# A hybrid S5, attention and MoE step on one core: dense part reordered, x2 rows kept on chip, expert outputs split

## The chip, the core and the metric

The kernel runs on one core of a Trainium2 chip. The metric is the device time of one execution in microseconds. The kernel before has a median of 2260.08 us over three runs (2256.23 to 2265.83). The profile is of one further execution.

## What is computed

One decoder layer in float32 for a prompt of 512 positions and 8 single-token samples, 520 tokens of width 2048 in all:

```python
u, q, k, v = split(rmsnorm(x) @ w_in)          # S5 channels 1024, q, k, v 1024 each
q, k = rope(q), rope(k)
# S5: 64 groups of 16 channels, each with 64 complex states
xs = scan(lambda_bar, B_bar u);  y = Re(C xs) + D u
z = gelu(y);  z = z * sigmoid(z @ w_glu)
# attention: three dilated windows, merged by their denominators
o = merge(branch(q, k, v, w, d) for (w, d) in ((128,1), (512,4), (2048,16)))
x = x + concat(rmsnorm(z), rmsnorm(o)) @ w_out
h = rmsnorm(x)                                 # MoE: best group of 4, best 2 of its 8 experts
x = x + sum_j gate_j * ((silu(h @ w_g[e_j]) * (h @ w_u[e_j])) @ w_d[e_j])
y = rmsnorm(x)
```

The samples attend to 1024 cached keys and values of which 256 positions count, and start from given states. k, v and the last states are outputs too.

## The kernel before

Everything lies in one SBUF tensor, `arena`, cut by hand into regions (A, R, W, U, Q, K, V, X), and in the eight PSUM banks, `ps`. So the profile calls every operand arena or psum, and the lines tell the work apart. Each engine has its own program, ordered by hand; semaphores tie them. SP issues nearly all DMAs, in program order: a wait in front of one holds all that follow.

**Input projection.** w_in comes in 32 column tiles of 1 MB through a ring of two slots (`load_w`, `load_tiles`). PE multiplies each with the 520 normed columns of x (`product`, line 497, 64 instructions a tile; float32 runs as two passes). Tiles 0 to 7 give u, which DVE evacuates (`u_out`, lines 1127 to 1129); 8 to 31 give q, k, v, which ACT copies out (lines 856 to 858) and GpSimd rotates (lines 1026 to 1028, 1031). Meanwhile DVE and ACT compute lambda and its powers (lines 1134 to 1192), and GpSimd the injection weights (`complex_product`, lines 997 to 1002), ended by `s_bw`.

**Injection and scan.** The sequence is cut into 128 chunks of 4. ACT issues DMAs that stack the weights of four rounds on the partitions (`stack_weights`, line 823, 16 DMAs a round, in two buffers) and u (lines 844, 845). PE runs rounds 0 and 1 behind tile 9, rounds 2 and 3 behind tile 11 (`inject`, line 534); ACT evacuates them (`chunk_states`, lines 833, 834), and issues the stacking of round 2 between the evacuations of rounds 0 and 1. Then DVE scans the 128 chunks, four small operations each (lines 1206 to 1211). After the scan it computes the samples' states, copies the samples' q doubled (line 1235), and multiplies and reduces cached keys in 8 chunks (lines 1247, 1248), for which SP loads one chunk beside each w_in tile from 22 on; the load of chunk c waits until DVE has used chunk c - 2. PE turns the doubled q into rows (line 556) between tiles 21 and 22.

**Attention and readout.** Scores, mask, exp, transposes and weighted values run by head and query tile (lines 575 to 591, 1259 to 1270). GpSimd computes the powers of the readout weights meanwhile. PE then forms the lag kernels (line 611) and for each of 8 channel tiles the readout: products with the lag kernels (line 623), then 64 instructions in which 128 states go into 32 output partitions (line 629), and the samples (lines 632, 636). ACT applies gelu (lines 907, 908). DVE works on the samples' attention: the score maximum by way of PE, exp on ACT in front of channel tile 3's gelu, then cached values in 8 chunks (lines 1307, 1308).

**Gate and norms.** Eight products with w_glu (line 497), sigmoid (920), z2 = u * sigmoid (1319), squares (914) summed over partitions with a matrix of ones (658). Then z's root (925), reciprocal (1329) and mix (1331), the z half of output tiles 0 and 1, squares and sums of o, its root (929), reciprocal (1333) and mix (1335).

**Output projection and routing.** 16 tiles of w_out; DVE adds x (line 1340). PE transposes x2 to token rows (689) and multiplies with the router (694). ACT copies the rows out (936), SP stores them in four parts to `x2_rows` in HBM (`store_x2`). DVE computes the choice of experts, positions and block tables in many small linked operations (lines 1370 to 1452); GpSimd zeroes two row buffers (1085) once the stores have landed.

**Experts.** Blocks of up to 64 token rows, one or more for each of 32 experts. GpSimd gathers rows from `x2_rows` (1067), ACT scales them (954), PE transposes (747), multiplies with gate and up (767) and with down (783); GpSimd scatters to `y_rows` (1078). SP loads each expert's six chunks of 2 MB (lines 453, 456); chunk i waits until PE has used chunk i of the expert before.

**Tail.** When all is scattered, SP reads both outputs of each token (line 477), after its x2 rows (474). For each of five token tiles DVE adds two weighted outputs (1494, 1495), ACT takes the root (975, 977), DVE norms (1489, 1490), SP stores (482).

The engines that run these instructions take the quoted waits in order; the one around which part of the change turns is PE's, between w_in tiles 21 and 22:

```python
            proj_pairs(6, 11)

            pe.wait_ge(s_ex, 1)
            pe.wait_ge(s_injev, 24)
            mm(ps[:, 4, 0:DH], smp_p[:, 0:P], ident, start=True, stop=True).then_inc(s_rows, 1)
            proj_pairs(11, 16)
```

## Time and profile before

| | |
|---|---|
| median of three runs | 2260.08 us (2256.23 to 2265.83) |
| profiled execution, its time | 2255.8 us |
| its span, first to last instruction | 2253.9 us |
| mean granted TensorE clock | 0.916 |
| PE busy | 1830.0 us, 81% |
| DVE, ACT, GpSimd busy | 590.0, 309.3, 276.7 us |
| DMA | 540.38 MB, mean 240 GB/s |
| chain that ended last | DMA 36%, PE 32%, DVE 5% |

PE is TensorE's matmuls, PEld its weight loads, DVE VectorE, ACT ScalarE, POOL GpSimd, SP SyncE; ACTq and SPq are the issuing sides. A row of instructions gives start, duration, engine, line, operation, output and input, count, and in brackets the idle time before it and what ended that. The granted clock (PEclk) is the share of full speed, 2.4 GHz; 0.50 is the lower level, 1.2 GHz. A chain row gives the time by which an instruction extended the chain, often less than its own duration.

### The profile page before, as it was taken

The numbers are of one execution on the slowest core, as the hardware profiler recorded it, in microseconds if no ns is written. First come the engines' busy times: TensorE is split into PE (matmuls) and PEld (weight loads), VectorE is DVE, ScalarE is ACT, GpSimd is POOL, SyncE is SP. The second block draws the span as 40 slices with busy tenths as digits, with TensorE's granted clock in tenths as the row PEclk, the third lists the DMA queues.
The fourth block names the chain that finished last, engine by engine and source line by source line (L and its number), as shares of the span: only waits on it lengthen the run. The fifth ranks groups of instructions, "written<-read, shape, count | busy, mean of one in ns | idle before, by whom it ended". The sixth has DMA issues, their size and how long they took to land.

```text
span 2253.9 us, 27087 instructions
## 1 busy us (share of the span) xinstructions
PE 1830.0 (81%) x10962; PEld 1288.7 (57%) x10963; DVE 590.0 (26%) x1201; ACT 309.3 (14%) x509; POOL 276.7 (12%) x193
## 2 busy tenths in 40 slices
PE   7798996899669989999498787777787797977870
PEld 6687885787338878888354444444444454544430
DVE  6700899431963421000410000000000010100006
ACT  3002110001231120111111110110110111111102
POOL 0731322101830000000100000000000000000000
PEclk9899998899779999999789999898998999999995
DMA  5153122234912412222599999999999879899977
GB/s 215 57 147 97 67 74 93 76 150 150 13 40 92 170 38 75 75 94 75 194 361 399 415 409 409 398 402 391 398 394 397 342 276 415 338 404 415 412 325 300
DMA packets 92403, 540.38 MB, mean 240 GB/s; under 512 B 28760, under 2 KB 41560, under 8 KB 47256
## 3 DMA queue, kind: packets, MB, share of 16 engines
q1 hardware_dynamic: 69920, 516.23, 60.6%
q0 software_dynamic: 7776, 17.07, 2.4%
q10 hardware_dynamic: 14656, 6.33, 1.3%
q8 instruction: 39, 0.64, 0.1%
q14 instruction: 12, 0.10, 0.0%
HBM read 522.04 MB, written 30.91 MB: 245 GB/s over the span
## 4 chain that ended last, share of the span: by engine, by line
DMA 36%; PE 32%; DVE 5%; issue 2%; ACT 1%; SPq 0%; POOLq 0%; ACTq 0%; DVEq 0%
DMA arena<-w_up_in 34%; PE psum L497 13%; PE psum L767 10%; PE psum L629 2%; PE psum L783 2%; DVE arena L1267 1%; PE psum L623 1%; DMA arena<-y_rows 1%; PE psum L747 1%; DVE arena L1261 1%; PE psum L658 1%; DVE arena L1490 1%; PE psum L694 1%; DVE arena L1259 1%; DMA arena<-x_rows,arena 0%
## 5 line engine op out<-in xcount | busy, mean ns | idle before, releaser
L497 PE MATMUL psum<-arena 128*128 128x260 f32 x3328 | 753.7, 390 | 39.1 <-ACT arena L805 12.3
L497 PEld LDWEIGHTS psum<-arena 128*128 128x128 f32 x3328 | 645.1, 194 | 143.5 <-issue 28.7
L767 PE MATMUL psum<-arena 128*64 128x256 f32 x4352 | 540.6, 407 | 175.4 <-DMA arena<-w_up_in 142.4
L767 PEld LDWEIGHTS psum<-arena 128*64 128x64 f32 x4352 | 332.4, 147 | 393.5 <-DMA arena<-w_up_in 166.5
L783 PE MATMUL psum<-arena 128*64 128x512 f32 x1088 | 249.8, 612 | 20.1 <-ACT arena L963 15.7
L1480 DVE TENSOR_TENSOR arena<-arena,psum 128x256 f32<-128x256 f32 x34 | 14.3, 421 | 956.8 <-PE psum L767 956.8
L783 PEld LDWEIGHTS psum<-arena 128*64 128x64 f32 x1088 | 77.2, 140 | 170.8 <-issue 138.7
L1078 POOL DMA_INDIRECT y_rows<-arena x34 | 34.1, 1002 | 982.5 <-ACT arena L968 933.6
L963 ACT ACTIVATE arena<-psum 128x256 f32<-128x256 f32 x34 | 13.1, 384 | 498.5 <-PE psum L773 498.5
L747 PE MATMUL psum<-arena 64*128 64x64 f32 x560 | 69.6, 276 | 13.6 <-ACT arena L954 13.6
L747 PEld LDWEIGHTS psum<-arena 64*128 64x128 f32 x560 | 64.8, 202 | 26.8 <-issue 26.8
L954 ACT ACTIVATE arena<-arena 64x2048 f32<-64x2048 f32 x35 | 69.8, 1995 | 27.6 <-DMA arena<-x_rows,arena 25.1
L968 ACT ACTIVATE arena<-psum 128x512 f32<-128x512 f32 x68 | 36.9, 594 | 259.2 <-PE psum L783 259.2
L1340 DVE TENSOR_TENSOR arena<-psum,arena 128x520 f32<-128x520 f32 x16 | 11.2, 700 | 223.4 <-PE psum L497 223.4
L1206 DVE TENSOR_TENSOR arena<-arena 128x64 f32<-128x64 f32 x128 | 42.5, 332 | 92.6 <-ACT arena L834 82.1
L1085 POOL MEMSET arena<- 128x2052 f32 x2 | 3.6, 1825 | 467.1 <-DMA x_rows<-arena 467.1
L1458 DVE TENSOR_TENSOR arena<-psum,arena 128x512 f32<-128x512 f32 x70 | 48.4, 692 | 34.4 <-PE psum L747 34.3
L856 ACT ACTIVATE arena<-psum 64x520 f32<-64x520 f32 x16 | 9.6, 601 | 313.5 <-PE psum L497 185.5
L1026 POOL TENSOR_TENSOR arena<-arena 128x520 f32<-128x520 f32 x16 | 20.8, 1301 | 247.4 <-ACT arena L858 176.2
L583 PE MATMUL psum<-arena 128*128 128x128 f32 x80 | 20.1, 365 | 35.6 <-DVE arena L1270 35.6
L1211 DVE TENSOR_TENSOR arena<-arena 128x64 f32 x128 | 47.4, 370 | 4.4
L629 PE MATMUL psum<-arena 128*32 128x128 f32 x512 | 47.7, 273 | 0.0
(284 smaller groups left out, 1221.9 us busy)
## 6 DMA issues: line engine op xcount, KB each, us to landing
arena<-w_gate_in SPq DMA_DIRECT2D x64, 2048.0 KB, 28.2
arena<-w_up_in SPq DMA_DIRECT2D x64, 2048.0 KB, 27.9
arena<-w_down_in SPq DMA_DIRECT2D x64, 2048.0 KB, 26.6
arena<-w_in_in SPq DMA_DIRECT2D x32, 1024.0 KB, 4.8
arena<-w_out_in SPq DMA_DIRECT2D x16, 1024.0 KB, 4.8
arena<-k_cache_in SPq DMA_DIRECT2D x8, 1024.0 KB, 6.8
arena<-v_cache_in SPq DMA_DIRECT2D x8, 1024.0 KB, 4.8
arena<-y_rows SPq DMA_DIRECT2D x4, 2048.0 KB, 17.8
```

Source lines behind the costliest of these rows:

```text
L497: last = mm(pair(n)[:, h, :], w(kk), rhs(kk)[:, HALF * h:HALF * (h + 1)], start=(kk == 0), stop=(kk == kn - 1 and stop))
L623: mm(yjc[b][:, lag:CHUNK, :], lagk[:, ct, lag, :], ujc[:, ct, 0:CHUNK - lag, :], start=(lag == 0), stop=False, skip_group_check=True)
L629: mm(yjc[b][32 * r:32 * r + 32, j, :], cw[:, j + 1, ri, i, :], xs[:, ri, i, 0:NCH], start=False, stop=(j == CHUNK - 1 and ri == 1), skip_g ...
L747: last = pe.transpose(ps[:, 3 + g, CAP * m:CAP * (m + 1)], rows[:, 8 * g + m, :], ident[0:CAP, 0:CAP])
L767: last = mm(ps[64 * h:64 * h + 64, i // 2, 0:256], xtr[:, kk, :], w[:, kk, 256 * h:256 * (h + 1)], start=(kk == 0), stop=(kk == 15))
L783: last = mm(ps[64 * h:64 * h + 64, 5 + b, :], act_col[:, kk % 2, 64 * (kk // 2):64 * (kk // 2) + 64], wd[:, kk, 1024 * h + 512 * b:1024 * ...
L954: A(xsc[0:CAP], xrow[j][0:CAP, 0:DM], ACT.Copy, scale=xrow[j][0:CAP, DM:DM + 1]).then_inc(s_sc_x, 1)
L968: A(yrow[:, 512 * b:512 * (b + 1)], ps[:, 5 + b, :], ACT.Copy).then_inc(s_yv, 1)
L1078: pool.indirect_dma_start(out=y_rows, out_offset=bass.IndirectOffsetOnAxis(ap=idx_now[:, 2 + j:3 + j], axis=0), in_=yrow, in_offset=None, ...
L1206: tt(scan_t[:, 0], column(it * 4 + s), lam_same, ALU.mult).then_inc(s_scan, 1)
L1211: tt(column(it * 4 + (s + 1)), scan_t[:, 2], scan_t[:, 1], ALU.add).then_inc(s_scan, 1)
L1458: tt(xtr[:, 8 * g:8 * g + 8, :], ps[:, 3 + g, :].rearrange("p (k n) -> p k n", n=CAP), gtab[:, 8 * g:8 * g + 8].unsqueeze(2).to_broadcast( ...
```

## The change

- **Lambda** (the small operations of lines 1173 to 1192, in new scratch) moves behind the last evacuation of u and the end of the injection weights, with the zeroing of the u stack, which stood before the last evacuation. ACT no longer waits for lambda before it stacks weights.
- **Stacking of rounds 2 and 3** is issued by SP, between w_in tiles 11 and 12, instead of by ACT.
- **The scan** is split into two loops of 16 turns; the samples' doubled q is copied between them.
- **Lag kernels and readout**: the loop over the four quarters of 32 output partitions becomes the innermost.
- **Norms**: squares are added on DVE (two buffers), and PE sums each norm once. o's squares, adds, sum, root, reciprocal and mix stand inside the gate products; output tiles 0 and 1 begin with their o half.
- **Experts' scratch** moves from R to A, so that the x2 rows stay on chip to the end. GpSimd zeroes only the four last columns of its row buffers, once the router's logits are done.
- **First expert**: down chunks 0 and 1 and gate chunk 1 are loaded behind w_out tiles 4, 8 and 12.
- **Outputs by lower and higher expert**: ids and gates are swapped where the first choice has the higher number. At the end the lower experts' outputs are loaded once all blocks before the last expert's are scattered and the last gate chunk is used, and are added to x2 at once; the higher ones follow after the last scatter, the tile of 8 rows first. x2 is not read back.

```diff
-            load_tiles(2, 8)
+            load_tiles(2, 6)
+            for rd in (2, 3):
+                sp.wait_ge(s_inj, 6 * (rd - 1))
+                for r in range(4):
+                    for j in range(CHUNK):
+                        sp.dma_start(bws[rd % 2][32 * j:32 * j + 32, :, r, :],
+                                     bw[32 * r:32 * r + 32, CHUNK - 1 - j, rd // 2, 4 * (rd % 2):4 * (rd % 2) + 4, :]
+                                     ).then_inc(s_bs[rd], 16)
+            load_tiles(6, 8)
...
+                if n in (4, 8, 12):
+                    if n == 4:
+                        sp.wait_ge(s_z, 8)
+                        sp.wait_ge(s_z2, 8)
+                        sp.wait_ge(s_out, 16 * 4)
+                    load_chunk({4: 4, 8: 5, 12: 1}[n], 0)
...
+            load_y(f_low, 0, 4, s_flow)
+            sp.wait_ge(s_gdone, more + NE)
+            for i in range(4):
+                load_y(f_low, 0, i, s_flow)
             sp.wait_ge(s_ddone, more + NE)
-            sp.wait_ge(s_x2st, 16 * 8)
             sp.dma_start(fg, t["g_final"].to_broadcast([P, DM])).then_inc(s_gf, 16)
-            for i, n in enumerate(TOKS):
-                sp.dma_start(fx[i][0:n], x2_rows[P * i:P * i + n, 0:DM]).then_inc(s_finl[i], 16)
             sp.wait_ge(s_sct, more * 16 + 16 * NE)
...
-                for r in range(4):
-                    i = 4 * ct + r
-                    for j in range(CHUNK):
-                        for ri in range(2):
+                for j in range(CHUNK):
+                    for ri in range(2):
+                        for r in range(4):
+                            i = 4 * ct + r
                             mm(yjc[b][32 * r:32 * r + 32, j, :], cw[:, j + 1, ri, i, :], xs[:, ri, i, 0:NCH],
                                start=False, stop=(j == CHUNK - 1 and ri == 1), skip_group_check=True)
...
+                if n == 6:
+                    sum_sq(ro, s_oad, 4, s_oss, 6)
...
-                outproj(n, 0, 8)
+                outproj(n, 8, 16, begin=8, stop=False)
                 if n == 0:
-                    pe.wait_ge(s_so, 1)
-                for m in range(4 * n, 4 * n + 4):
-                    sum_sq(m, s_osq, s_oss, 6)
+                    sum_sq(rz, s_zad, 7, s_zss, 4)
...
+                if n == 4:
+                    act.wait_ge(s_so, 1)
+                    for h in range(2):
+                        A(v[:, 4 * h:4 * h + 4, :], q[:, 4 * h:4 * h + 4, :], ACT.Square).then_inc(s_osq, 1)
+                if n == 6:
+                    act.wait_ge(s_oss, 1)
+                    A(halves(ro), ps[:, 6:8, 0:HALF], ACT.Sqrt, bias=eps, scale=1.0 / (8 * P)).then_inc(s_ort, 1)
...
+            pool.wait_ge(s_lg, 1)
+            for j in range(2):
+                pool.memset(xrow[j][:, DM:XW], 0.0).then_inc(s_z0, 1)
+            pool.wait_ge(s_z0, 2)
             pool.wait_ge(s_x2st, 16 * 8)
-            for j in range(2):
-                pool.memset(xrow[j], 0.0).then_inc(s_z0, 1)
-            pool.wait_ge(s_z0, 2)
...
+            scan(0, NCH // 8)
+            dve.wait_ge(s_rope, 8)
+            doubled(smp_p[:, 0:P], sample(q)).then_inc(s_ex, 1)
+            scan(NCH // 8, NCH // 4)
...
+            def z_add(n):
+                dve.wait_ge(s_zsq, n + 1)
+                if n >= 2:
+                    dve.wait_ge(s_zad, n - 1)
+                tt(rz, rz, glu_q[:, n % 2], ALU.add).then_inc(s_zad, 1)
...
+                if n == 4:
+                    dve.wait_ge(s_osq, 2)
+                    tt(v[:, 0:4], v[:, 0:4], v[:, 4:8], ALU.add).then_inc(s_oad, 1)
+                    dve.wait_ge(s_oad, 1)
+                    tt(v[:, 0:2], v[:, 0:2], v[:, 2:4], ALU.add).then_inc(s_oad, 1)
+                    dve.wait_ge(s_oad, 2)
+                    tt(ro, v[:, 0], v[:, 1], ALU.add).then_inc(s_oad, 2)
+                if n == 6:
+                    dve.wait_ge(s_ort, 1)
+                    link(dve.reciprocal(ro, ro))
+                    for c in range(8):
+                        stt(q[:, c], q[:, c], gao[:, c:c + 1], ro, ALU.mult, ALU.mult).then_inc(s_mix, 1)
...
+            dve.wait_ge(s_flow, 16 * 5)
+            for i, n in enumerate(TOKS):
+                stt(fx[i][0:n, 0:DM], f_low[i][0:n], gate_w[0:n, i, 0:1], fx[i][0:n, 0:DM], ALU.mult, ALU.add
+                    ).then_inc(s_fadd, 1)
```

## Rows read from the trace of the kernel before

**Rows 1.** Busy time by stage (columns in its first line; x counts instructions).

```profile
core 0: us, PE busy (x) PEld busy (x) DVE busy (x) ACT busy (x) POOL busy (x), PEclk, DMA share, GB/s
...
372.00:405.00 33.00, 0.28 (x2) 0.15 (x1) 29.73 (x109) 1.80 (x3) 3.80 (x3) 0.54 0.17 64
...
749.50:849.00 99.50, 88.93 (x387) 74.33 (x387) 22.22 (x27) 18.01 (x30) 0.00 (x0) 0.97 0.22 83
...
1133.00:2192.50 1059.50, 864.41 (x6052) 479.47 (x6052) 67.94 (x177) 127.05 (x169) 65.61 (x67) 0.94 0.96 385
2192.50:2253.90 61.40, 0.00 (x0) 0.00 (x0) 35.34 (x20) 13.86 (x18) 1.00 (x1) 0.54 0.75 298
```

**Rows 2.** Chain that ended last, in the expert stage (start us, us, what).

```profile
1604.44 26.60 DMA arena<-w_up_in
```

**Rows 3.** Waits, 80 to 420 us (us in total, times, longest us).

```profile
PE psum L556 <- DVE arena L1235: 32.7, 1, 32.7
...
PE psum L497 <- DVE arena L1129: 12.3, 1, 12.3
...
PE psum L534 <- ACT arena L834: 8.3, 1, 8.3
```

**Rows 4.** Instructions in order of time, 0 to 178 us.

```profile
92.33 2.32 DVE L1187 COPY arena<-arena 128x32 f32<-128x32 f32 x1
...
168.71 0.63 ACTq L845 DMA_DIRECT2D arena<-arena  x1
```

**Rows 5.** DMA issues by tensor (KB each, median us from issue to landing).

```profile
arena<-k_cache_in SPq DMA_DIRECT2D x8, 1024.0 KB, 6.8
...
arena<-arena ACTq DMA_DIRECT2D x4, 8.0 KB, 3.1
```

**Rows 6.** Groups of instructions by line and shape, 665 to 749 us.

```profile
L629 PE MATMUL psum<-arena 128*32 128x128 f32 x512 | 47.7, 273 | 0.0
L629 PEld LDWEIGHTS psum<-arena 128*32 128x32 f32 x512 | 45.4, 109 | 1.1
L1307 DVE TENSOR_TENSOR arena<-arena 128x2048 f32<-128x2048 f32 x8 | 18.3, 2288 | 1.1 <-DMA arena<-v_cache_in 1.0
```

**Rows 7.** Chain that ended last, 660 to 705 us.

```profile
665.40 3.73 PE psum L611 x128
...
679.36 5.89 PE psum L629 x64
```

**Rows 8.** Chain that ended last, 748 to 870 us.

```profile
771.47 0.88 PE psum L658 x4
772.35 7.01 PE psum L497 x32
...
815.40 3.41 DVE arena L1329
...
819.75 9.93 PE psum L497 x32
...
844.82 3.41 DVE arena L1333
```

**Rows 9.** Instructions in order of time, 1040 to 1180 us.

```profile
1105.55 3.59 POOL L1085 MEMSET arena<- 128x2052 f32 x2 [467.14 <-DMA x_rows<-arena]
1105.59 1.80 DVE L1403 TENSOR_SCALAR arena<-arena 128x32 f32<-128x32 f32 x1
...
1118.81 2.07 POOL L1067 DMA_INDIRECT arena<-x_rows,arena  x1 [9.66 <-DVE arena L1443]
...
1128.41 2.00 ACT L954 ACTIVATE arena<-arena 64x2048 f32<-64x2048 f32 x1 [25.08 <-DMA arena<-x_rows,arena]
```

**Rows 10.** Instructions in order of time, 2140 us to the end.

```profile
2204.03 2.19 SPq L477 DMA_DIRECT2D arena<-y_rows  x5
2215.18 2.35 DVE L1494 SCALAR_TENSOR_TENSOR arena<-arena 128x2048 f32<-128x2048 f32 x1 [31.63 <-DMA arena<-y_rows]
...
2248.62 2.34 DVE L1490 SCALAR_TENSOR_TENSOR arena<-arena 8x2048 f32<-8x2048 f32 x1
```

More of the change, by code:

```diff
@@ L492, in _, with product @@
             mm = pe.matmul
-            def product(n, w, rhs, k0, kn, stop=True):
+            def product(n, w, rhs, k0, kn, stop=True, begin=0):
                 for kk in range(k0, kn):
@@ L497, in product @@
                         last = mm(pair(n)[:, h, :], w(kk), rhs(kk)[:, HALF * h:HALF * (h + 1)],
-                                  start=(kk == 0), stop=(kk == kn - 1 and stop))
+                                  start=(kk == begin), stop=(kk == kn - 1 and stop))
                 return last
@@ L607, in _ @@
             pe.wait_ge(s_msk, 4 * NH)
[L608 to L609 removed]
+            for ct in range(8):
                 for ri in range(2):
[L611 to L613 removed]
+                    for r in range(4):
+                        last = mm(ps[32 * r:32 * r + 32, ct // 4, P * (ct % 4):P * (ct % 4 + 1)].rearrange(
+                            "p (j m) -> p j m", j=CHUNK), bst[:, ri, 4 * ct + r, :], cw[:, 0:CHUNK, ri, 4 * ct + r, :],
+                            start=(ri == 0), stop=(ri == 1))
             last.then_inc(s_lag, 1)
@@ L653, in _, with sum_sq @@
             pe.wait_ge(s_ptev, 4 * NH)
-            def sum_sq(n, squares, done, banks):
-                pe.wait_ge(squares, n + 1)
+            def sum_sq(src, added, count, done, banks):
+                pe.wait_ge(added, count)
                 for h in range(2):
-                    last = mm(ps[:, banks + h, 0:HALF], ones, glu_q[:, n % 2, HALF * h:HALF * (h + 1)],
-                              start=(n == 0), stop=(n == 7))
+                    last = mm(ps[:, banks + h, 0:HALF], ones, src[:, HALF * h:HALF * (h + 1)], start=True, stop=True)
                 last.then_inc(done, 1)
@@ L908, in _, with z_square @@
                 A(u[:, ct, SEQ:T], ps[:, 2 * (ct % 2) + 1, 0:NS], ACT.Gelu_apprx_tanh).then_inc(s_z, 1)
-            def squares(n, src, ready, count, freed, freed_at, done):
-                act.wait_ge(ready, count)
-                if freed_at > 0:
-                    act.wait_ge(freed, freed_at)
-                A(glu_q[:, n % 2], src[:, n, :], ACT.Square).then_inc(done, 1)
+            def z_square(n):
+                act.wait_ge(s_z2, n + 1)
+                if n == 0:
+                    act.wait_ge(s_out, 16 * 4)
+                if n >= 3:
+                    act.wait_ge(s_zad, n - 2)
+                A(glu_q[:, n % 2] if n else rz, z2[:, n, :], ACT.Square).then_inc(s_zsq, 1)
             for n in range(8):
@@ L921, in _ @@
                 if n >= 1:
-                    squares(n - 1, z2, s_z2, n, s_zss, n - 2, s_zsq)
-            squares(7, z2, s_z2, 8, s_zss, 6, s_zsq)
-            act.wait_ge(s_zss, 8)
+                    z_square(n - 1)
+                if n == 4:
[5 more added lines that the diff above has]
+                    A(halves(ro), ps[:, 6:8, 0:HALF], ACT.Sqrt, bias=eps, scale=1.0 / (8 * P)).then_inc(s_ort, 1)
+            z_square(7)
+            act.wait_ge(s_zss, 1)
             A(halves(rz), ps[:, 4:6, 0:HALF], ACT.Sqrt, bias=eps, scale=1.0 / (8 * P)).then_inc(s_zrt, 1)
-            for n in range(8):
-                squares(n, q, s_so, 1, s_oss, n - 1, s_osq)
-            act.wait_ge(s_oss, 8)
-            A(halves(ro), ps[:, 6:8, 0:HALF], ACT.Sqrt, bias=eps, scale=1.0 / (8 * P)).then_inc(s_ort, 1)
             for b in range(20):
@@ L1194, in _ @@
-            dve.wait_ge(s_bw, 1)
+            dve.wait_ge(s_bw, 1)
+            r1, i1 = lre[:, 1024:NP], lim[:, 1024:NP]
+            dve.tensor_copy(lamp[:, 0], r1)
+            dve.tensor_copy(lamp[:, 1], i1)
+            dve.tensor_copy(coef[:, 0], cre[:, 1024:NP])
+            link(dve.tensor_copy(coef[:, 1], cim[:, 1024:NP]))
+            dve.memset(ust[:, :, :, NCH:136], 0.0).then_inc(s_zu, 1)
+            a, b = stat[:, 0:32], stat[:, 32:64]
+            c, d = (region("vsamp", 64)[:, 32 * j:32 * j + 32] for j in range(2))
@@ new lines, in _ @@
+            e, f = lam_same[:, 0], lam_cross[:, 0]
+            for _ in range(2):
+                tt(a, r1, r1, ALU.mult)
+                link(tt(b, i1, i1, ALU.mult))
+                link(tt(d, r1, i1, ALU.mult))
+                link(tt(c, a, b, ALU.subtract))
+                link(ts(d, d, 2.0, None, ALU.mult))
+                dve.tensor_copy(e, c)
+                link(dve.tensor_copy(f, d))
+                r1, i1 = e, f
+            dve.tensor_copy(lam_same[:, 1], e)
+            ts(lam_cross[:, 1], f, -1.0, None, ALU.mult).then_inc(s_ldve, 1)
@@ L1331, in _ @@
                 stt(z2[:, n], z2[:, n], gso[:, n:n + 1], rz, ALU.mult, ALU.mult).then_inc(s_mix, 1)
-            dve.wait_ge(s_ort, 1)
-            link(dve.reciprocal(ro, ro))
-            for n in range(8):
-                stt(q[:, n], q[:, n], gao[:, n:n + 1], ro, ALU.mult, ALU.mult).then_inc(s_mix, 1)
             dve.wait_ge(s_x2l, 16)
```

243 lines of the change are left out of this document (121 added, 122 removed).

## The prediction

> **What bounds the kernel now.** I read the stages first, then the chain that ended last, then the waits, then the instructions in order of time around each wait. The expert stage is 1059.5 of 2253.9 us, with the DMA engines 96% busy at 385 GB/s [rows 1]; its chain alternates some 27 us of waiting for expert weights with some 5 us of PE work [rows 2]. The diff changes nothing in that loop, so it must shift as a block; only what lies before and after it can win. The dense part, up to 1088 us, is PE's except where PE waits: the three waits of [rows 3], and the norms, where a stage of 99.5 us has 88.9 us of PE [rows 1]. The tail of 61.4 us after the last matmul has none [rows 1].
>
> **A. Start, lines 1166 to 1192 and 818 to 862.** Today DVE's chain of 128x32 operations for lambda stands between two evacuations of u. GpSimd computes meanwhile, and an operation of 0.2 us takes 2.32 us [rows 4]; PE waits 12.3 us [rows 3]. Moved behind all of u, the chain has cover: PE projects until inject. But the injection also needs the stacked u, issued by ACT behind 32 weight DMAs: last issue at 168.71 us [rows 4], landing 3.1 us later [rows 5], so 171.8 us. Inject began at 172.9 us. Of 12.3 us only 1.1 us is won; the rest becomes a wait for those DMAs. The zeroing of ust now follows the last u evacuation and four copies, near 132 us, before ACT is free at 152 us: nothing. Rounds 2 and 3 of the weight stacking, 32 DMAs, go from ACT to SP. ACT's 16 issues of round 2 held back its evacuations, for which PE waited 8.3 us [rows 3]; that goes. On SP they stand before the w_in tiles 12 to 15. At the 0.6 us per issue of ACT, 32 take 20 us, from about 177 to 197 us; tile 12 is needed about 218 us and loads in under 7 us: covered. Without cover each late microsecond is PE's. One idle of 11 us stands for two of 12.3 and 8.3 us, so the slow clock after an idle is paid once: 0.4 us. Together 9.8 us, bounds 7 to 13.
>
> **B. Sample queries in mid-scan.** PE waits 32.7 us at line 556 for a copy that DVE makes after the scan [rows 3]; in that stretch the granted clock is 0.54 [rows 1], nearly all at the lower of its two levels, 1.2 GHz, and the first tile after it takes 15.9 instead of 14.0 us. The copy needs only head 8's rope, done some 20 us before mid-scan, and costs DVE 0.16 us. What is late next: SP issues w_in tile 25 behind the load of cached keys 2, which waits until DVE has used chunk 0, after the scan. From the scan's end (about 392 us, moved with A) that is 3.1 us of states, 0.3 of copy and two operations of 2.29 (the like of the cached values' in [rows 6]): 400.1 us. Tile 25 lands 6.8 us [rows 5] plus an issue of 0.7 later, 407.6 us, when PE has been free since 405.2: a wait of 2.4 us, and 2.0 us for the clock after it. Won: 32.7 + 1.8 - 2.4 - 2.0 = 30.1 us, bounds 26 to 34.5. Later loads are fast enough for tiles of 14 us.
>
> **C. Readout quarters in turn.** Eight channel tiles run 64 pieces each at line 629 in 5.89 us [rows 7], 92 ns a piece, ordered so that 16 pieces in a row write the same 32 output partitions. Line 611 has the same shape, turns to another quarter every 4 pieces, and runs 128 in 3.73 us [rows 7], 29 ns a piece. With quarters in turn I take the value of line 611: 64 x 29 = 1.87 us, 4.0 us less, times 8 = 32.2 us. Line 611 itself has little left. Bounds: nothing, and all of it. Cover: each tile's gelu on ACT (1.3 us) fits in the new 4.8 us. DVE's sample values (8 x (2.29 + 2.29) us, [rows 6]) start when ACT has done its exp, after tile 3; that moves forward by only half of the gain. They end at 736 us on today's scale, the gate products start at 717 us and need z only from product 4 on, at about 745 us, the sample sum at 738.5 us: 2.6 us to spare.
>
> Beside this stands a rule of the Trainium skill, page "TensorE: Matmul & The Clock Gate", section "The mechanism": a weight load overlaps a running matmul only when its row group differs. All these pieces use all 128 rows, so by it the loads (512 x 109 ns = 55.8 us, [rows 6]) would be the floor and the readout 8.7 us longer. The 29 ns of line 611, with loads of the same shape, speak against it.
>
> **D. Norms inside the gate products.** Today the stage costs 99.5 us [rows 1]: 8 products, 16 sums of squares of 0.88 us, and twice a root, a reciprocal of 3.41 us and the first mix before PE continues, 5 us each; after the first, 32 pieces take 9.93 instead of 7.01 us [rows 8], the slower clock. New: 8 products and 2 halves at 7.01, 2 sums at 0.88, small pieces 0.7: 72.7 us. Is DVE's and ACT's share covered? From the end of product 4 (t = 0): two squares of half the o rows 1.94 us each, to 5.2; DVE's adds 4.3, to 9.5; PE's sum at 14.9; root 17.3; reciprocal 20.7, eight mixes 26.2; z's last add 28.3. PE reaches z's sum at 29.6 and the z half of output tile 0 at 37.5, when z's mix has begun at 35.3. All covered, with 1.3 us as the smallest margin. Won 26.8, and 1.9 for the clock after the second idle: 28.7 us, bounds 20 to 31.
>
> **E. Routing.** GpSimd's zeroing of the two row buffers (3.59 us) ran over two tiny DVE operations, one of 1.80 us instead of 0.18 [rows 9], the next alike: 3.3 us on the path. Now it zeroes 4 columns earlier. DVE gains four tiny operations before the positions, where it waited 0.6 us: 0.3 us. Gate weights' six extra operations are off the path. Won 3.0 us, bounds 1 to 4. Three of expert 0's six chunks are loaded during the output projection. The stream is not shortened by that, as expert 1's chunks wait for PE on expert 0; but the first gather (issued 1118.81, used 1128.41, [rows 9]) shares the engines with 6.3 MB less: I take 4 us, bounds 0 to 6. On SP the chunks stand ahead of w_out tiles that have 14 us: nothing.
>
> **F. Tail.** Today y is read (8.5 MB) behind x2 (4.2 MB): issue 2204.03, first use 2215.18 us, then 15 operations of 2.35 us [rows 10]. New: x2 stays; the lower rows are loaded under the last block and added before the last scatter lands; the higher rows are 4.2 MB. DVE is free for them at about 2202.5 us (lower rows in at 2190.5, five adds of 2.35); then ten operations of 2.35, 24.0 us with reciprocals, 1.5 us for the first root, and the store of a full 1 MB tile instead of 8 rows, at most 5.4 us: 2233 us. If the last scatter still lands at 2204, 2237 us. Won 17 to 21, I take 20; bounds 13 to 24.
>
> **Sum.** 9.8 + 30.1 + 32.2 + 28.7 + 3.0 + 4.0 + 20 = 127.8 us off the profiled execution's 2255.8: 2128.0 us. The median of the runs stands 4.3 us above it, so I forecast 2132 us.
>
> **Rivals.**
> (1) The quarters overlap no further, or loads take turns. For it: the 109 ns loads. Against: line 611. Without C the time is 2164 us; with loads as the floor 2173 us.
> (2) A wait takes the place of one removed: DVE's sample values reach into the gate products (spare 2.6 us), or the 1.3 us in D is missed, or keys on SP hold more than one w_in tile. For it: DVE is in order and has three narrow places; against: the sums above. Worth 10 to 25 us: 2150 us.
> (3) The earlier chunks do shorten the weight stream. For it: [rows 1], 96% busy, and 6.3 MB are 15 us at 400 GB/s. Against: the engines fall idle before expert 1 is asked for. Then 2117 us.
> (4) Slower than before: changing quarter makes PE finish each piece before the next load. Place: line 629 alone. Price: 109 + 273 ns [rows 6] for 512 pieces is 196 us instead of 47, so 2132 + 32 + 149 = 2313 us. The other parts win 95.6 us, so it decides from 279 ns a piece. Against: 32 such changes within 3.73 us at line 611.
> (5) The moved copy doesn't free PE, since another condition of line 556 is as late: B's gain lost, 2162 us. Against: injection is evacuated 170 us earlier.
>
> **Numbers.** About 0.5% is what a measurement of this kernel can tell from no change, 11 us. Chances: forecast 0.70, (1) 0.07, (2) 0.14, (3) 0.04, (4) 0.01, (5) 0.02, and 0.02 for a surprise in the expert stage that eats all. The bounds of A to F, taken together, give 2112 to 2150 around the forecast; with (2), 2112 to 2158. Faster 0.97, same 0.01, slower 0.02.
>
> **What would show it.** The wait at line 556 gone and one of 2 to 3 us at a w_in tile near 405 us; the wait for DVE at line 1129 replaced by 11 us before inject; 64 readout pieces in 1.9 us and PE busy through the gate products without the two 5 us gaps; DVE's two 1.8 us operations short; output tile 0 finished about 100 us earlier; an expert stage of 1055 to 1062 us, 107 us earlier; a tail of about 41 us. Wrong if the expert stage lengthens by what the dense part won, if readout pieces stay near 92 ns, or if DVE shows in PE's waits after the readout.

## The result, and the profile after

The changed kernel takes 2148.06 us (median of four runs, 2141.37 to 2154.72), where the kernel before took 2258.15 us beside it: a ratio of 0.951, 95% interval 0.947 to 0.955. The forecast was 2132 us in a range of 2112 to 2158. The profiled execution, at 2141.37 us the fastest of the four, has a span of 2139.6 us, 114.3 us under that of before, where the working said 127.8.

The stages of the profile after (busy time by stage, columns in its first line) answer to [rows 1]:

```profile
core 0: us, PE busy (x) PEld busy (x) DVE busy (x) ACT busy (x) POOL busy (x), PEclk, DMA share, GB/s
0.00:219.20 219.20, 188.92 (x901) 164.27 (x902) 63.45 (x87) 39.34 (x78) 67.54 (x37) 0.97 0.42 132
219.20:515.30 296.10, 285.51 (x1282) 246.20 (x1282) 203.59 (x532) 28.19 (x47) 64.19 (x50) 0.98 0.28 102
515.30:643.20 127.90, 78.34 (x369) 45.85 (x369) 103.35 (x235) 43.74 (x86) 72.59 (x34) 0.74 0.58 56
643.20:685.10 41.90, 40.69 (x727) 30.50 (x727) 21.08 (x21) 11.86 (x20) 0.00 (x0) 0.96 0.34 129
685.10:759.20 74.10, 73.40 (x332) 62.69 (x333) 48.23 (x47) 19.39 (x24) 0.00 (x0) 1.00 0.41 157
759.20:1013.70 254.50, 243.00 (x1201) 210.86 (x1201) 21.73 (x58) 26.57 (x64) 0.14 (x2) 0.96 0.30 103
1013.70:1035.20 21.50, 3.71 (x48) 3.23 (x48) 14.45 (x42) 2.71 (x2) 2.91 (x2) 0.50 0.65 270
1035.20:2091.80 1056.60, 858.47 (x6052) 476.48 (x6052) 68.48 (x182) 126.69 (x169) 65.48 (x67) 0.95 0.97 389
2091.80:2139.60 47.80, 0.00 (x0) 0.00 (x0) 34.99 (x20) 13.75 (x18) 1.00 (x1) 0.55 0.55 216
```

The same boundaries in both traces give the gain of each part. Each is the start, or where its name says so the end, of the same PE instruction, and the last is the end of the span. A gain is what the distance between two boundaries lost.

| boundary | before | after | gain since the last | forecast |
|---|---|---|---|---|
| w_in tile 12 starts | 229.9 | 219.2 | A 10.7 | 9.8 |
| transposes of attention start | 549.6 | 515.3 | B 23.5 | 30.1 |
| readout starts | 675.5 | 643.2 | -1.8 | 0 |
| gate products start | 749.6 | 685.1 | C 32.1 | 32.2 |
| output projection ends | 1087.6 | 997.3 | D 25.8 | 28.7 |
| first expert product | 1133.3 | 1035.2 | E 7.9 | 7.0 |
| last expert product ends | 2192.5 | 2091.8 | 2.5 | 0 |
| end | 2253.9 | 2139.6 | F 13.6 | 20 |

The waits of the same profile (us in total, times, longest us) stand where [rows 3] stood:

```profile
PE psum L565 <- issue: 13.7, 1, 13.7
PE psum L528 <- DMA arena<-w_in_in: 8.6, 1, 8.6
...
PE psum L528 <- ACT arena L948: 0.7, 1, 0.7
```

The three waits of before are gone. One of 13.7 us, in front of the injection, and one of 8.6 us, for a w_in tile, have come. The second was forecast at 2.4 us, and it is where most of B's miss lies. The instructions around it in order of time (start us, us, instruction, idle before it and what ended that):

```profile
361.45 42.25 PE L528 MATMUL psum<-arena 128*128 128x260 f32 x192
412.28 28.03 PE L528 MATMUL psum<-arena 128*128 128x260 f32 x115 [8.59 <-DMA arena<-w_in_in]
...
391.84 1.27 DVE L1237 TENSOR_TENSOR arena<-arena 128x64 f32<-128x64 f32 x1
393.03 1.37 DVE L1239 TENSOR_TENSOR arena<-arena 128x64 f32<-128x64 f32 x1
394.44 1.33 DVE L1241 TENSOR_TENSOR arena<-arena 128x64 f32 x1
395.80 0.27 DVE L1236 TENSOR_TENSOR arena<-arena 128x64 f32<-128x64 f32 x1
...
391.67 1.35 POOL L1058 TENSOR_TENSOR arena<-arena 128x520 f32<-128x520 f32 x1 [10.12 <-ACT arena L885]
...
404.81 0.34 SPq L382 DMA_DIRECT2D arena<-k_cache_in  x1
405.35 0.33 SPq L376 DMA_DIRECT2D arena<-w_in_in  x1
```

PE runs from 361.45 to 403.7 us without a stop, past the query rows. SP issues tile 25 only at 405.35 us, behind the load of cached keys, which waits for VectorE to finish the scan and its first key products. The tile lands at 412.28. The scan itself ran late: a VectorE operation of 0.27 us takes 1.27 to 1.37 us when it meets one of GpSimd's rotations.

In the tail (same view) stand the lines that answer to [rows 10]:

```profile
2072.57 2.59 SPq L499 DMA_DIRECT2D arena<-y_rows  x5
...
2101.87 2.44 SPq L499 DMA_DIRECT2D arena<-y_rows  x5
...
2098.61 11.39 DVE L1545 SCALAR_TENSOR_TENSOR arena<-arena 128x2048 f32<-128x2048 f32 x5 [15.27 <-DMA arena<-y_rows]
2110.03 4.60 DVE L1560 SCALAR_TENSOR_TENSOR arena<-arena 8x2048 f32<-8x2048 f32 x2
```

The lower experts' rows are asked for at 2072.57 us, 19 us before the last expert product ends, but VectorE starts on them 6.8 us after that end. In the chain that ended last (start us, us, what) the last of their five loads lands just before that start:

```profile
2074.74 23.85 DMA arena<-y_rows
```

From there VectorE works almost without a gap to 2135 us.

### The profile page after: what moved, and what is told of

Its sections match the earlier page's. It is cut to its first block, busy times and chain, and to the rows that moved or that the text cites. A ratio compares the mean times of both kernels' runs of the same rounds, so it can differ in the third digit from the quotient of the medians.

```text
span 2139.6 us, 26995 instructions
## 1 busy us (share of the span) xinstructions
PE 1772.0 (83%) x10906; PEld 1240.1 (58%) x10907; DVE 579.4 (27%) x1218; ACT 312.2 (15%) x505; POOL 273.9 (13%) x193
## 4 chain that ended last, share of the span: by engine, by line
DMA 37%; PE 30%; DVE 6%; issue 2%; ACT 1%; SPq 0%; POOLq 0%; ACTq 0%; DVEq 0%
DMA arena<-w_up_in 35%; PE psum L528 13%; PE psum L797 10%; PE psum L813 2%; DVE arena L1300 1%; DMA arena<-y_rows 1%; PE psum L654 1%; DVE arena L1294 1%; DVE arena L1292 1%; PE psum L660 1%; PE psum L777 1%; PE psum L722 1%; DVE arena L1552 1%; DVE arena L1545 0%; DMA y_rows<-arena 0%
## 5 line engine op out<-in xcount | busy, mean ns | idle before, releaser
L528 PE MATMUL psum<-arena 128*128 128x260 f32 x3328 | 744.8, 387 | 26.5 <-ACT arena L835 13.0
L528 PEld LDWEIGHTS psum<-arena 128*128 128x128 f32 x3328 | 639.1, 192 | 128.3 <-issue 19.3
L797 PE MATMUL psum<-arena 128*64 128x256 f32 x4352 | 538.9, 406 | 178.5 <-DMA arena<-w_up_in 142.0
L813 PE MATMUL psum<-arena 128*64 128x512 f32 x1088 | 245.4, 603 | 20.4 <-ACT arena L994 15.6
L1236 DVE TENSOR_TENSOR arena<-arena 128x64 f32<-128x64 f32 x128 | 43.3, 338 | 92.9 <-ACT arena L862 82.6
L1239 DVE TENSOR_TENSOR arena<-arena 128x64 f32<-128x64 f32 x128 | 47.4, 371 | 0.0
```

What stands on the lines that cost most here:

```text
L528: last = mm(pair(n)[:, h, :], w(kk), rhs(kk)[:, HALF * h:HALF * (h + 1)], start=(kk == begin), stop=(kk == kn - 1 and stop))
L797: last = mm(ps[64 * h:64 * h + 64, i // 2, 0:256], xtr[:, kk, :], w[:, kk, 256 * h:256 * (h + 1)], start=(kk == 0), stop=(kk == 15))
L813: last = mm(ps[64 * h:64 * h + 64, 5 + b, :], act_col[:, kk % 2, 64 * (kk // 2):64 * (kk // 2) + 64], wd[:, kk, 1024 * h + 512 * b:1024 * ...
L1236: tt(scan_t[:, 0], column(it * 4 + s), lam_same, ALU.mult).then_inc(s_scan, 1)
L1239: tt(scan_t[:, 2], scan_t[:, 0], column(it * 4 + (s + 1)), ALU.add).then_inc(s_scan, 1)
```

## The experiments

Twelve runs follow, of eleven kernels (`no_preload` and `no_early_chunks` are the same one). Eight have one execution each, the four with a ratio below have five, beside a kernel before with a median of 2257.47 us. The changed kernel did not run beside those four; it is compared with them by its own ratio of 0.951, interval 0.947 to 0.955. The expert loop, the same code everywhere, took between 1056.0 us (the changed kernel) and 1064.2 us in the fourteen traces, from the start of its first product to that of its last, so a single time tells nothing under some 8 us. The stages do, and where they and a single time differ, the stages decide.

### The copy back behind the scan (part B)

The second half of the scan stands in front of the copy of the samples' q (and of `s_ex`, which frees PE) and not behind it:

```diff
+            scan(NCH // 8, NCH // 4)
...
-            scan(NCH // 8, NCH // 4)
```

> The changed kernel, with the samples' doubled q copied after the second scan loop instead of between the two; the split of the scan stays. Theory (GpSimd's rope shares the scan's time): the scan grew from 173.1 to 179.1 us because PE no longer stops, so that the rope operations of two or three more tiles run under it. Then here, where PE waits again from tile 21 on, the scan is back at 173 us (within 1.5), PE waits 30 to 33 us at the sample rows, the 8.6 us wait at w_in tile 25 is gone, and attention's first transpose starts 23 to 26 us later than the 515.4 us of the changed kernel. Rival (the second loop costs it): the scan stays at 179 us and PE waits some 6 us longer, 38 us.

Measured: 2161.18 us, 19.8 us more than the changed kernel's profiled execution. The transposes start at 534.6 instead of 515.3 us, 19.3 later, so the loss is in part B's stage, but less than the 23 to 26 us expected. Waits of PE in this kernel:

```profile
PE psum L587 <- DVE arena L1248: 29.7, 1, 29.7
```

The long wait is back, with 29.7 us instead of 32.7, and the wait of 8.6 us for tile 25 isn't there: SP had time. That both figures fall short by about 3 us fits the edit: the copy stands right behind the scan here (the query rows start at 390.2 us, the scan ends at 390.0), while the kernel before first computes the samples' states, 3.1 us, and only then copies. The scan shows the second thing. Each line below is the stretch from the first to the last operation of the scan, of the kernel with the copy behind it, the changed kernel and the kernel before, in this order (columns as above):

```profile
216.70:390.00 173.30, 142.22 (x640) 122.67 (x640) 158.52 (x513) 21.30 (x36) 46.21 (x36) 0.91 0.22 76
```

```profile
217.60:396.70 179.10, 177.53 (x803) 153.67 (x804) 164.47 (x513) 24.91 (x42) 53.89 (x42) 0.99 0.22 80
```

```profile
228.40:401.60 173.20, 142.22 (x640) 122.68 (x640) 158.37 (x513) 21.25 (x36) 46.22 (x36) 0.91 0.21 76
```

VectorE runs the same operations of the scan. With the copy in mid-scan PE goes on to further tiles under the scan, GpSimd rotates two of them there (42 operations instead of 36), and the scan is 5.8 us longer, 1.0 us for each of the six. The other traces agree: the scan takes 172.6 to 173.3 us in the three with 36 operations of GpSimd under it, and 178.5 to 179.2 us in the eleven with 42. The wait that was removed had kept GpSimd quiet.

### The order of the readout (part C)

The readout of the changed kernel turns to another column quarter every 2 instructions. Three kernels change only the length of these runs. To 16, the order of before:

```diff
-                for j in range(CHUNK):
-                    for ri in range(2):
-                        for r in range(4):
-                            i = 4 * ct + r
+                for r in range(4):
+                    i = 4 * ct + r
+                    for j in range(CHUNK):
+                        for ri in range(2):
```

To 8:

```diff
-                for j in range(CHUNK):
-                    for ri in range(2):
-                        for r in range(4):
+                for jj in range(0, CHUNK, 2):
+                    for r, j, ri in [(r, j, ri) for r in range(4) for j in (jj, jj + 1) for ri in range(2)]:
```

To 4:

```diff
-                    for ri in range(2):
-                        for r in range(4):
+                    for r in range(4):
+                        for ri in range(2):
```

> The changed kernel, with the readout's loops in the old order (16 instructions in a row for one quarter of the output partitions); the lag kernels keep the new order. Theory (only runs on the same quarter are serial): 64 pieces take 5.9 us instead of 1.9, the readout stage 74 instead of 42.1 us, and the gate products start 32 us later; the DVE spare of the samples' values grows and nothing else changes: 32 us on the whole. Rival (the moved work covers part of it): the gate stage gives some back, and the whole is less than 27 us slower.

> The changed kernel, with the readout's pieces ordered so that 8 instructions in a row (two positions, two parts, two passes) go to one quarter before the next. Theory (a piece overlaps only with neighbours of other quarters, within a window of few instructions): between 29 and 92 ns a piece, by the count of serial neighbours about 7/8 of a serial piece, so 64 pieces in 4.5 to 5.9 us. Rival (the window is deep, and only the number of changes counts): near 1.9 to 2.8 us.

> The changed kernel, with 4 instructions in a row for a quarter (both parts, two passes), as line 611 had before. Theory: as line 611 had it, 29 to 30 ns a piece, 64 pieces in 1.9 us, and the readout stage within 1 us of 42.1. Rival (the full turn after every logical product is needed): over 2.5 us for 64 pieces.

Measured: 2172.76, 2160.81 and 2143.05 us. The old order costs 31.4 us on the whole and 31.9 us in the readout, as the theory had it. In the traces 64 instructions take (changed kernel, then runs of 4, 8 and 16; instructions in order of time):

```profile
662.16 1.96 PE L660 MATMUL psum<-arena 128*32 128x128 f32 x64
```

```profile
661.31 2.03 PE L660 MATMUL psum<-arena 128*32 128x128 f32 x64
```

```profile
660.61 4.33 PE L659 MATMUL psum<-arena 128*32 128x128 f32 x64
```

```profile
662.07 5.96 PE L660 MATMUL psum<-arena 128*32 128x128 f32 x64
```

The 4.33 us of the runs of 8 lie between what rival (up to 2.8) and theory (from 4.5) allowed: both ranges were missed, the theory's by little. Divided by 64: 31 ns a piece in runs of 2, 32 in runs of 4, 68 in runs of 8, 93 in runs of 16. So it is the length of the run in one quarter that matters, with next to nothing lost up to 4 and, at 8, some 60% of what 16 costs ((68 - 31) / (93 - 31)). Why a long run is slow, no run shows. The loads of line 660 in groups by line and shape (count, busy us, mean ns of one, idle us before), in the changed kernel and then with runs of 16:

```profile
L660 PEld LDWEIGHTS psum<-arena 128*32 128x32 f32 x512 | 13.5, 109 | 1.0
L660 PEld LDWEIGHTS psum<-arena 128*32 128x32 f32 x512 | 45.4, 109 | 1.1
```

A load has 109 ns in both, but together they fill 13.5 us in one and 45.4 in the other: in the short runs they overlap each other, so their duration sets no floor. Runs of 4 were line 611's pattern [rows 7], and its value was the right one to take. The rule of the Trainium skill that the prediction weighed (page "TensorE: Matmul & The Clock Gate", section "The mechanism": a load overlaps only when its row group differs) would, taken alone, make all four orders equally slow; the four traces disagree with it. The same section also lets a load go ahead of running matmuls when it targets the background weight buffer; whether that is what happens here, no run shows.

### The readout's order alone, in the kernel before

```diff
-                for r in range(4):
-                    i = 4 * ct + r
-                    for j in range(CHUNK):
-                        for ri in range(2):
+                for j in range(CHUNK):
+                    for ri in range(2):
+                        for r in range(4):
+                            i = 4 * ct + r
```

> The kernel before with the order of the readout alone changed (part C): the four column quarters one after the other, piece by piece. The theory expects what the forward comparison gave, 32 us off: about 2228 us where the kernel before takes 2260, with the 128 x 32 pieces at about 30 ns each instead of 93. The rival (the gain of 32 us needs the other edits, for VectorE or the copies behind the readout would be the bound in the kernel before) expects 2235 to 2250 us, with TensorE waiting for VectorE in that stage.

Measured: 2228.02 us beside 2260.33, 32.3 less, and 27.8 less than the profiled execution of before. Instructions in order of time:

```profile
685.27 1.96 PE L629 MATMUL psum<-arena 128*32 128x128 f32 x64
```

The forecast value again, 31 ns. The readout takes 43.6 us where it took 74.1, 30.5 less. But the first expert product comes only 25.8 us earlier (1107.5 against 1133.3). VectorE's cached values are now late for the samples' sum, which they were not in the kernel before:

```profile
PE psum L672 <- DVE arena L1310: 4.2, 1, 4.2
```

So the rival is right in kind and small: 4.2 us are given back in the norms. The stages from the gate products to the end of the output projection take 6.5 us more than in the kernel before; the other 2.3 us were not traced to a cause. In the changed kernel, whose 74 us of gate products have no such wait, they have cover.

### The stacks back on ScalarE (part A)

SP's 32 issues for rounds 2 and 3, behind w_in tile 11, are left out, and ScalarE issues them between its evacuations:

```diff
-                    chunk_states(0)
-                    chunk_states(1)
+                    for rd in range(2):
+                        chunk_states(rd)
+                        stack_weights(rd + 2)
```

> The changed kernel with the stacks of the injection issued by ScalarE again, as before. The theory of part A (ScalarE's queue held the stacks behind its other issues, and the first two injections waited for them) expects TensorE's waits of about 9.8 us around the first injections to come back and the rest to stand: about 2151 us beside 2141. The rival (the gain of part A came from the shorter operations around it, not from the queue) expects 2141 to 2144 us.

Measured: 2157.52 us, 16.2 more. The transposes start 8.9 us later (524.2 against 515.3), the first expert product 9.1 later (1044.3); the other 7 us lie in the expert loop, 1062.8 against 1056.0 us, which the edit doesn't touch and which is inside that loop's spread. Waits of PE, then ScalarE's instructions in order of time:

```profile
PE psum L558 <- issue: 11.4, 1, 11.4
PE psum L558 <- ACT arena L857: 8.3, 1, 8.3
```

```profile
176.13 9.75 ACTq L846 DMA_DIRECT2D arena<-arena  x15
185.92 0.49 ACT L856 ACTIVATE arena<-psum 128x384 f32<-128x384 f32 x1 [9.85 <-issue]
```

The wait of 8.3 us of [rows 3] is back to the tenth. From the start of the injection to that of w_in tile 12 it takes 58.4 us here, 57.0 in the kernel before and 47.2 in the changed kernel, so the stacks' move carries at least 9.8 of A's 10.7 us. The other 0.9 us, by which the injection starts earlier than in the kernel before, can't be told from chance: with the same code up to there it starts between 169.4 and 172.2 us in the twelve traces with the change.

### GpSimd's zeroing back beside the routing (part E)

```diff
+            pool.wait_ge(s_x2st, 16 * 8)
-                pool.memset(xrow[j][:, DM:XW], 0.0).then_inc(s_z0, 1)
+                pool.memset(xrow[j], 0.0).then_inc(s_z0, 1)
...
-            pool.wait_ge(s_x2st, 16 * 8)
```

> The changed kernel with GpSimd's zeroing put back beside VectorE's two small operations of the routing. The theory of part E expects these two to take about 1.8 us each again instead of 0.18 (3.3 us together) and the end to be as much later: about 2144.5 us. The rival (they were long for a wait in their own operands, not for GpSimd) expects 0.18 us each and 2141 us.

Measured: 2144.31 us, 2.9 more. From the routing's first product (line 758) to the first expert product it takes 24.8 us, and 21.5 in the changed kernel: 3.3 more, as expected. Not two operations are long, as expected, but one, from GpSimd's start to GpSimd's end:

```profile
1012.65 0.18 DVE L1456 TENSOR_SCALAR arena<-arena 128x32 f32<-128x32 f32 x1
1012.87 3.62 DVE L1457 TENSOR_SCALAR arena<-arena 128x32 f32<-128x32 f32 x1
1012.90 3.55 POOL L1118 MEMSET arena<- 128x2052 f32 x2 [408.96 <-DMA x_rows<-arena]
```

By the Trainium skill (page "SBUF — State Buffer", section "SBUF: two separate sides") VectorE and GpSimd share a pair of ports, and one of them holds it for its whole instruction while the other is blocked; of VectorE's operations this concerns those in a mode that uses both ports and, against a GpSimd operation that reads SBUF, those with two inputs there. The trace agrees with the blocking, 3.62 us beside 3.55; of which kind line 1457 is, no run shows.

### Without the early chunks (part E)

```diff
-                if n in (4, 8, 12):
...
-                    load_chunk({4: 4, 8: 5, 12: 1}[n], 0)
-            for i in (0, 2, 3):
+            for i in range(6):
                 load_chunk(i, 0)
```

The first expectation names the edit badly: what is left out are the three early loads of weights shown here, and x2 stays on chip. Its numbers are meant for them.

> The changed kernel without what keeps the x2 rows on chip ahead of the first expert: the first gathered tile comes from its indirect DMA alone. The theory of part E expects the first expert's first matmul to come 3 to 5 us later (the gather's 9.6 us of before in place of 4.8), and the end as much later: about 2145 us. The rival (the time from first to last expert is set by the weight stream, which began at its own time) expects the later start to be taken back by the end: 2141 us, with the first expert shorter by as much.

> The changed kernel without the three early loads of expert weights: all six chunks of the first expert are asked for after the output projection, as before. One look of it gave 2153.6 us. Theory one (the early chunks help only the first gather, 4.0 us in part E) expects a ratio to before of 0.953. Theory two (they also shorten the stream of weights by some 8 us, the fourth rival's thought in part) expects 0.956 to 0.957, and in the trace again 8 us more from the first to the last matmul of the experts than the 1056 us of the changed kernel.

Measured: 2153.57 us in one execution; 2152.96 us as median of five others (2146.51 to 2156.66), a ratio of 0.953, interval 0.950 to 0.955. Theory one's figure was met, theory two's lies outside. The interval overlaps the changed kernel's, so the medians alone don't show a loss; the traces do. Line 758 to the first expert product takes 27.1 us in both traces instead of 21.5: the gather costs 5.6 us more, where part E took 4.0. The rows of the gather, second trace, then changed kernel:

```profile
1025.03 1.97 POOL L1095 DMA_INDIRECT arena<-x_rows,arena  x1 [19.95 <-DVE arena L1492]
...
1035.49 2.00 ACT L981 ACTIVATE arena<-arena 64x2048 f32<-64x2048 f32 x1 [22.87 <-DMA arena<-x_rows,arena]
```

```profile
1025.42 1.97 POOL L1099 DMA_INDIRECT arena<-x_rows,arena  x1 [19.92 <-DVE arena L1496]
...
1030.24 2.00 ACT L985 ACTIVATE arena<-arena 64x2048 f32<-64x2048 f32 x1 [17.21 <-DMA arena<-x_rows,arena]
```

From issue to use 10.5 us against 4.8. Whether the loop gains too stays open. Its two traces show 1064.2 and 1063.8 us, more than the ten with early chunks (1056.0 to 1062.8), but the kernel before, whose chunks are also late, has 1058.5 us, and with its readout changed 1056.6. What is not there are the 15 us of rival (3).

### The cached keys one tile pair later

```diff
-            load_tiles(8, 11)
-            load_tiles(11, 12, 11)
-            load_tiles(12, 15, 11)
-            load_tiles(15, 16)
+            load_tiles(8, 12)
+            load_tiles(12, 13, 12)
+            load_tiles(13, 16, 12)
```

All eight loads of cached keys move two tiles back. The first that waits for VectorE now stands in front of w_in tile 27, not tile 25.

> The changed kernel (ratio to before 0.951, 2148 us) with the second load of cached keys put behind w_in tile 27 instead of tile 25 on SyncE's queue, so that no weight tile of the projection stands behind a load that waits for the end of the scan. The theory expects TensorE's wait of 8.6 us at tile 25 and the 2.9 us of slower clock after it to go, and nothing in their place: 11 us less, a ratio of 0.946. The rival (the keys, asked for later, are now late for the scores, or VectorE is) expects a new wait of TensorE between 510 and 640 us, and a ratio of 0.949 to 0.952.

Measured: 2132.14 us (2129.97 to 2136.84), a ratio of 0.944, interval 0.942 to 0.946. The transposes start at 503.1 us, 12.2 earlier than in the changed kernel (0.8 of them were there at tile 12 already), and PE runs through (order of time; then busy time by stretch):

```profile
399.65 50.57 PE L527 MATMUL psum<-arena 128*128 128x260 f32 x230
```

```profile
396.00:412.00 16.00, 16.00 (x75) 13.87 (x74) 14.61 (x14) 0.60 (x1) 1.28 (x1) 1.00 0.35 132
```

Of the waits in 400 to 520 us only those of attention are left, and from 510 to 640 us, where the rival looked for a new one, PE waits for the same four things as in the changed kernel. In this trace, the slowest of its five runs, the loop takes 1062.6 us, so the profile alone would have shown 4.5 us; the first expert product comes 11.0 us earlier.

### The lower rows one by one (part F), and both edits together

```diff
-                load_y(f_low, 0, i, s_flow)
+                load_y(f_low, 0, i, s_gw[i])
...
-            dve.wait_ge(s_flow, 16 * 5)
-            for i, n in enumerate(TOKS):
+            for i in (4, 0, 1, 2, 3):
+                n = TOKS[i]
+                dve.wait_ge(*((s_flow, 16) if i == 4 else (s_gw[i], 48)))
```

> The changed kernel with VectorE's five additions of the lower experts' rows waiting each for its own load, not all for the last of the five. The theory of the tail (VectorE bounds it from the landing of the lower rows on) expects the first two to four additions, 2.3 us each, to be done before the last load lands: 5 to 6 us less in the tail, a ratio of 0.9485. The rival (the five loads share the engines with the last expert's weights and land nearly together) expects the additions to begin less than 2 us earlier and a ratio of 0.950 to 0.951.

Measured: 2139.96 us (2137.67 to 2140.88), ratio 0.947, interval 0.945 to 0.950. Order of time:

```profile
2092.45 11.39 DVE L1546 SCALAR_TENSOR_TENSOR arena<-arena 8x2048 f32<-8x2048 f32 x5 [6.51 <-issue]
2109.22 2.34 DVE L1561 SCALAR_TENSOR_TENSOR arena<-arena 8x2048 f32<-8x2048 f32 x1 [5.38 <-DMA arena<-y_rows]
```

The additions start 2.3 us before the last expert product ends (2094.8), not 6.8 after: 9 us earlier. But 5.4 of them become a wait for the higher rows, which SP asks for at 2106.41 us, when the last scatter has landed. The tail is 44.0 us instead of 47.8, so the trace carries 3.8 us, less than the 5 to 6 expected; the ten traces with the changed kernel's tail have 46.9 to 48.0. The 8.1 us between the medians are within what the two intervals leave open.

> Both edits together, the keys behind tile 27 and a wait for each load of lower rows. They lie in stages that share nothing, so the theory expects the sum of the two: about 16 us less than the changed kernel, a ratio of 0.944, which is below both kernels. The rival (what the dense part wins is given back in the expert stage, which goes at the pace of the weights) expects the ratio of the changed kernel, 0.951, less the tail's part.

Measured: 2129.91 us (2126.14 to 2130.92), ratio 0.9425, interval 0.940 to 0.945, the lowest of all. The first expert product starts 12.1 us earlier than in the changed kernel and the tail is 4.0 us shorter, at 43.8: the sum of 16 us that was expected. The loop takes 5.6 us more in this trace. It beats the changed kernel and the kernel before; against the later keys alone it is 2.2 us ahead in the medians, which the intervals don't separate.

## Why the prediction was right, and where it wasn't

**A, right.** 10.7 us against 9.8. Inject starts at 171.98 us (forecast 171.8), behind 13.7 us of waiting. In the trace the last stacked piece of u has landed at 171.89, and in all twelve traces with the change the injection starts 0.1 us after that landing, so an earlier evacuation of u would not have shortened the wait: ScalarE issues the stacking of u only behind its weight DMAs. That the start was met to 0.2 us is in part luck, as it lies anywhere from 169.4 to 172.2 us in them. SP's 32 issues took 21.86 us, from 177.50, with no wait of PE behind them:

```profile
177.50 21.86 SPq L391 DMA_DIRECT2D arena<-arena  x32
```

**B, the mechanism right, a term mis-sized.** The wait of 32.7 us went, and the one named as its successor came, at the tile named, for the reason named. The step that failed is "a wait of 2.4 us, and 2.0 us for the clock after it". It measured 8.6 us, and 2.9 for the clock: the tile behind it took 16.9 us instead of 14.0. Tile 25 was to land at 407.6 us and came at 412.3. The working took the scan's end as moved with A alone. In fact the scan lost 5.8 us to GpSimd's rotations that PE's progress now brought under it: of A's 10.7 us only 4.9 came through to its end (396.7 after 401.6). That is shown by putting the copy back. Moving the key loads won back the wait and the clock behind it, 11.5 us: part B's stage took 284.8 us instead of 296.2.

**Attention, minus 1.8 us, not foreseen, and not the change's.** Its transposes took 5.38 us instead of 3.71, at a granted clock of 0.68 where the kernel before had 1.00; nothing in the diff touches them. They take 3.71 us in six of the fourteen traces and 5.38 in eight. The kernel with runs of 16 is the changed kernel up to there, and it has 3.71 us and an attention stage of 124.9 us beside 127.8. Over all traces the stage takes 124.9 to 129.1 us.

**C, right.** 32.1 against 32.2, confirmed in both directions: the readout is 31.9 us longer when the order is undone in the changed kernel (73.9 against 42.0), and 30.5 shorter when it alone is changed in the kernel before. Rivals (1) and (4) fall with it.

**D, nearly.** The stage took 74.1 us and 72.7 were forecast. The two 5 us gaps are gone and both norms have their cover. ScalarE's sigmoid was not in the sum, and PE waits 0.7 us for it (line 948). The first router products after the first output tiles take 5.47 us instead of 4.03, again the clock (0.70 over them, 1.00 before). Together with the gate stage's 1.4 us that is the 3 us missed, and the clock's part is not the change's: in the kernel with runs of 4, the same from the readout on, these products take 4.03 us, and from the first gate product to the end of the output projection it takes 308.7 us where the changed kernel takes 312.1 and 309.2 were forecast. (The terms of the 72.7 us add up to 72.6.)

**E, right in sum.** 7.9 against 7.0: the zeroing 3.3 (forecast 3.3) and the gather 5.6 (4.0), by the two runs that undo them. That leaves minus 1.0 for the added small operations (forecast minus 0.3), a remainder that no run isolates. The stretch from line 758 on takes 21.3 to 22.9 us in the nine traces in which nothing of it is undone, so each of these terms is uncertain by about 1 us.

**F, mis-sized.** 13.6 instead of 20 us. The step that failed is "lower rows in at 2190.5", 2 us before the last product ended. In the trace the last of five loads is in 6.8 us after it. They were asked for while the last expert's weights, 4 MB of w_down among them, were still on their way (the last chunk landed at 2088.1 us), and VectorE waited for all five. With a wait for each, VectorE starts 1.9 us after the last chunk of w_down has landed (2092.45 and 2090.6 us), and then waits for the higher rows instead. The run with a wait for each load shows the bound behind: the prediction's second case, "if the last scatter still lands at 2204, 2237 us", is a tail of 44.5 us, and that kernel's is 44.0.

**Sum.** B 6.6, D 2.9, F 6.4 and attention 1.8 are missing, 17.7 us; A, E and the expert loop gave 4.3 more. With C's 0.1 that makes 13.5 of 127.8 us. The median is 16 us above the forecast's 2132, because it also stands 6.7 us above the profiled execution, where the forecast took the 4.3 of the kernel before. The loop's 2.5 us lie within its spread of 8 us. Rival (2) described what happened in kind, a wait in the place of one removed, at SP's queue, and larger than the forecast's own case; but that wait and the clock behind it cost 7.1 us more than was put for them, not the 10 to 25 of the rival. That the median of 2148 lies beside its 2150 is luck: the other 9 us come from elsewhere, from the tail above all. Rival (3) is not borne out, and rival (5) fell.

## What to carry to other kernels

When a wait goes, list what ran slowly or not at all during it, on every engine: here the freed engine fed another, and that one slowed the chain which set the next transfer. A load that waits for something late should not stand in a queue in front of loads that don't; here a place two tiles later was worth 16 of the changed kernel's 2148 us in the medians, 11 of them seen in the trace. For rows that come in several transfers, wait for each: 3.8 us of the tail here.

## What the hardware showed

- Small PE instructions with 32 output columns cost 31 or 32 ns a piece in runs of 2 or 4 in one column quarter, 68 in runs of 8 and 93 in runs of 16, with the same 109 ns of load each.
- A 128x32 operation of VectorE, 0.18 us otherwise, lasted 3.62 us over GpSimd's 3.55 us of zeroing; in the scan each GpSimd operation of 1.3 us cost VectorE 1.0 us.
- The expert loop, with the DMA engines busy throughout, spread over 1056 to 1064 us between executions of the same loop, wider than the error of any part.
